# Adaptive-norm scale and shift: from broadcast rows to per-partition scalars at the transposed eviction

## The reference

```python
mod = jax.nn.silu(c) @ w_ada + b_ada
sh1, sc1, g1, sh2, sc2, g2 = [m[:, None, :] for m in jnp.split(mod, 6, axis=-1)]
h = rmsnorm(x, ln_mix_g) * (1.0 + sc1) + sh1
z = h @ w_in
...
x = x + g1 * ((ga * oa + gb * ob + gc * oc) @ w_out)
h2 = rmsnorm(x, ln_ffn_g) * (1.0 + sc2) + sh2
f = moe(h2, router_w, router_b, moe_w1, moe_b1, moe_w2, moe_b2)
x = x + g2 * f
```

## Time and profile before

| what | value |
|---|---|
| median of three runs | 1684.28 us |
| the runs | 1684.28, 1681.4, 1685.1 us |
| span of the profiled execution | 1684.8 us |
| PE busy, share of the span | 1590.9 us, 94% |
| DVE, ACT, POOL busy | 489.1 (29%), 317.7 (19%), 105.6 us (6%) |
| mean granted TensorE clock | 0.962 |
| DMA | 491.89 MB, 292 GB/s over the span |

### The profile page before, as it was taken

The page is one execution under the profiler, slowest core; times in us unless marked ns, Lnnn a source line. Parts: engine busy times, 40 slices in busy tenths (PEclk is TensorE's granted clock), DMA queues, the critical chain, the costliest instruction groups (busy, mean ns, idle before and its releaser), DMA issues.

```text
span 1684.8 us, 20411 instructions
## 1 busy us (share of the span) xinstructions
PE 1590.9 (94%) x8125; PEld 696.9 (41%) x8126; DVE 489.1 (29%) x824; ACT 317.7 (19%) x582; POOL 105.6 (6%) x107
## 2 busy tenths in 40 slices
PE   4989898979999888899999999999999999999996
PEld 4455555444565656233333333333333333333332
DVE  2141222266024645322222222222122222222224
ACT  1123332112121133111111111111111111111120
POOL 0000000112113433000000000000000000000000
PEclk8989999989999888999999999999999999999999
DMA  9462532233223363599999999999593999999993
GB/s 361 170 253 100 204 146 85 103 110 106 94 85 131 103 218 113 221 418 429 429 428 428 429 428 429 429 429 428 244 419 155 417 424 429 428 429 429 428 428 140
DMA packets 38583, 491.89 MB, mean 292 GB/s; under 512 B 4784, under 2 KB 4912, under 8 KB 9744
## 3 DMA queue, kind: packets, MB, share of 16 engines
q1 hardware_dynamic: 34144, 477.27, 68.5%
q0 software_dynamic: 4400, 14.06, 2.9%
HBM read 486.99 MB, written 4.33 MB: 292 GB/s over the span
## 4 chain that ended last, share of the span: by engine, by line
PE 88%; DVE 4%; DMA 4%; ACT 2%; POOL 1%; issue 1%; SPq 0%; DVEq 0%; POOLq 0%
PE ps L1592 28%; PE ps L1264 17%; PE ps L1621 14%; PE ps L1555 6%; PE ps L1541 6%; PE ps L1200 4%; PE ps L1271 4%; DMA ring<-in_w_dense 2%; PE ps L1216 1%; PE ps L1223 1%; PE ps L1597 1%; DMA out_sample_retention<-V 1%; PE ps L1322 1%; PE ps L1342 1%; PE ps L1467 1%
## 5 line engine op out<-in xcount | busy, mean ns | idle before, releaser
L1592 PE MATMUL ps<-ring,arena 128*64 128x512 f32 x2176 | 480.2, 594 | 2.8 <-issue 2.8
L1264 PE MATMUL ps<-ring,xT 128*128 128x512 f32 x672 | 313.0, 624 | 2.9 <-DMA ring<-in_w_dense 2.1
L1592 PEld LDWEIGHTS ps<-ring,arena 128*64 128x64 f32 x2176 | 156.5, 137 | 308.3 <-issue 305.7
L1621 PE MATMUL ps<-ring,arena 128*64 128x512 f32 x1088 | 248.5, 599 | 0.0
L1264 PEld LDWEIGHTS ps<-ring,xT 128*128 128x128 f32 x672 | 131.4, 200 | 165.1 <-issue 160.8
L1178 DVE TENSOR_TENSOR U<-ps,U 128x1024 f32<-128x1024 f32 (+1 forms) x102 | 124.4, 1219 | 248.8 <-PE ps L1555 248.8
L1621 PEld LDWEIGHTS ps<-ring,arena 128*64 128x64 f32 x1088 | 72.0, 137 | 168.1 <-issue 142.3
L1555 PE MATMUL ps<-arena 64*128 64x512 f32 x420 | 119.6, 636 | 0.8 <-ACT arena L734 0.8
L1541 PE MATMUL ps<-T,arena 128*64 128x512 f32 (+1 forms) x420 | 104.4, 616 | 1.2 <-DVE arena L1068 1.2
L1169 DVE TENSOR_SCALAR arena<-ps 128x512 f32<-128x512 f32 x34 | 23.5, 692 | 217.4 <-PE ps L1597 217.4
L707 ACT ACTIVATE W<-ps 128x512 f32<-128x512 f32 x35 | 21.0, 599 | 338.5 <-PE ps L1541 338.5
(11 more groups left out here) (258 smaller groups left out, 1122.9 us busy)
## 6 DMA issues: line engine op xcount, KB each, us to landing
ring<-in_w_moe SPq DMA_DIRECT2D x192, 2048.0 KB, 14.8
ring<-in_w_dense SPq DMA_DIRECT2D x33, 2048.0 KB, 8.8
V<-in_state POOLq DMA_DIRECT2D x8, 256.0 KB, 5.7
out_sample_retention<-V POOLq DMA_DIRECT2D x8, 256.0 KB, 3.1
R<-in_x_prompt SPq DMA_DIRECT2D x1, 1024.0 KB, 16.6
arena<-in_cache_kT POOLq DMA_DIRECT2D x8, 128.0 KB, 3.7
arena<-in_cache_v POOLq DMA_DIRECT2D x8, 128.0 KB, 3.7
arena<-in_b_gate POOLq DMA_DIRECT2D x4, 256.0 KB, 4.0
```

Of the source, the lines that this page charges most:

```text
L1264: last = mm(banks[t][0], xT[:, k, t * P:t * P + P], wv[:, k, :], start=(k == 0), stop=(k == KD - 1))
L1592: last = mm(ps[64 * a:64 * a + 64, half, :], xgT[:, k, j % 2, :], wv[:, k, HALF * a:HALF * a + HALF], start=(j % 2 == 0 and k == 0), stop= ...
L1621: last = mm(ps[64 * a:64 * a + 64, 2, :], actT[:, k, j - 4, :], wv[:, k, HALF * a:HALF * a + HALF], start=(j == 4 and k == 0), stop=(j == ...
```

## The change

Scale and shift are no longer spread to rows. The root still multiplies the token rows, and this scaled x is transposed at once, without gain or shift. Two new transposes per pair of `ada` units (`turn_modulation`) put the model dimension of scale and shift on partitions, and `take_modulation` adds bias and gain there: 128 partitions x 8 chunks x 9 conditions. In the transposed layout the scale and shift of the prompt are one number per partition and chunk. ScalarE (Identity with scale and bias) and VectorE (TENSOR_SCALAR) apply them while they evict the transposed x from PSUM. The sample tile has eight conditions, so VectorE multiplies and adds broadcast views there (`modulated_sample`). `project` takes the chunks in the order in which they are evicted.

SP loads the input, the identity and the parameters ahead of the second unit; bias rows and gain rows are not loaded any more at the start (the bias of the two gates comes later on POOL's queue). The norm before the experts works likewise. Since the gather wants token rows, `xT` is transposed back into `T` (24 transposes, six copies). The spreads of the second gate move from ahead of the expert count to behind the positions.

```diff
-AUX = ["ada2", "ada3"] + [f"gain0{x}" for x in HALVES] + ["ada0", "ada1"] + [f"shift0{x}" for x in HALVES]
-AUX += ["ada4", "ada5", "kT0", "kT1", "kT2"]
+AUX = ["ada2", "ada3", "ada0", "turned2", "ada1", "turned0", "ada4", "ada5", "kT0", "kT1", "kT2"]
 for _t in range(2):
     AUX += [f"qT{_t}{q}" for q in range(4)]
     for _g in range(KVH):
         AUX += [f"sc{_t}{_g}{k}" for k in range(_t + 1)]
+        AUX += {(0, 2): ["turned6"], (1, 0): ["turned8"]}.get((_t, _g), [])
...
+    HAT_BANKS = [1, 3, 0, 2]
+    FIRST_CHUNKS = [4, 5, 6, 7, 0, 1, 2, 3]
+    FFN_BANKS = [1, 3, 0, 2, 4]
+    BACK_BANKS = [(0, 4), (1, 3), (2, 0)]
...
-        for j in range(4):
-            sp.dma_start(mod_bias[32 * j:32 * j + 32], ins["b_ada"][j].partition_broadcast(32)).then_inc(mod_bias_in, 16)
-        load_unit(1)
         sp.dma_start(R[:, 0:2, :], ins["x_prompt"].rearrange("(t p) d -> p t d", p=P)).then_inc(x_in, 16)
         sp.dma_start(R[0:64, 2, :], ins["x_sample"]).then_inc(x_in, 16)
-        sp.dma_start(consts[:, 0:FIRST_CONSTS], ins["consts"][:, 0:FIRST_CONSTS]).then_inc(select_in, 16)
-        sp.dma_start(ln_gain, ins["ln_mix_g"].partition_broadcast(P)).then_inc(ln_mix_in, 16)
+        sp.dma_start(consts[:, 0:IDENT_COLS], ins["consts"][:, 0:IDENT_COLS]).then_inc(ident_in, 16)
+        sp.dma_start(params[:, :], ins["params"]).then_inc(params_in, 16)
+        load_unit(1)
         load_unit(2)
         load_unit(3)
         load_unit(4)
...
+        aux_filled(pool, "ada1")
+        for j in range(4):
+            pool.dma_start(mod_bias[32 * j:32 * j + 32], ins["b_ada"][j].partition_broadcast(32)).then_inc(mod_bias_in, 16)
...
-        take_transposed(0, TR_NORM)
+        act.wait_ge(hat_turned, 1)
+        act.wait_ge(shift_ready, 1)
+        for k in (4, 5, 0, 1):
+            A(xT[:, k, 0:SEQ], ps[:, HAT_BANKS[k // 2], (k % 2) * SEQ:(k % 2 + 1) * SEQ], ACT.Identity,
+              bias=shift_mix[:, k, 0:1], scale=gain_mix[:, k, 0:1]).then_inc(hT_act, 1)
...
-        for x in HALVES:
-            name = f"shift1{x}"
-            aux_filled(act, name)
-            cols = slice(HALF * int(x[1]), HALF * int(x[1]) + HALF)
-            if x[0] == "s":
-                A(T[0:64, 2, cols], aux_bank(name)[0:64], ACT.Copy).then_inc(used(name), 1)
-            else:
-                A(T[:, 0, cols], aux_bank(name), ACT.Copy)
-                A(T[:, 1, cols], aux_bank(name), ACT.Copy).then_inc(used(name), 1)
+        take_transposed(TR_LATER, 4)
+        def take_ffn(t):
+            for q in (2 * t, 2 * t + 1):
+                act.wait_ge(ffn_turned, q + 1)
+                k0 = TR_LATER[q][1]
+                for m in range(4):
+                    last = A(xT[:, k0 + m, t * P:t * P + P], ps[:, FFN_BANKS[q], m * P:m * P + P], ACT.Identity,
+                             bias=shift_ffn[:, k0 + m, 0:1], scale=gain_ffn[:, k0 + m, 0:1])
+                last.then_inc(ffnT_ready, 1)
         for t, pieces in enumerate((2, 1, 1)):
             take_pieces(pieces)
-            if t == 2:
-                take_transposed(2, TR_LATER, 0, 4)
             act.wait_ge(x1_ready, t + 1)
             A(W[0:ROWS[t], t, :], R[0:ROWS[t], t, :], ACT.Square, accum_out=stat[0:ROWS[t], t:t + 1]).then_inc(squared, 1)
             sqrt_of(stat[:, t:t + 1], 12 + t)
-        take_transposed(2, TR_LATER, 4)
+            if t:
+                take_ffn(t - 1)
+        for t, r in enumerate(ROWS):
+            for h in range(2):
+                act.wait_ge(back_turned, 2 * t + h + 1)
+                A(T[0:r, t, HALF * h:HALF * h + HALF], ps[0:r, BACK_BANKS[t][h], :], ACT.Copy).then_inc(back_ready, 1)
...
+            if n in gate_rows:
+                g = gate_rows[n]
+                X.tensor_tensor(mod[:, g, :], aux_bank(name)[:, 0:128], mod_bias[:, g, :], ALU.add).then_inc(used(name), 1)
+            else:
+                X.tensor_copy(mod_rows[:, n % 2, :], aux_bank(name)[:, 0:128]).then_inc(used(name), 1)
+        def take_modulation(n, out, gain=None):
+            name = f"turned{n}"
+            aux_filled(dve, name)
+            turned = aux_bank(name)[:, 0:256].rearrange("p (k b) -> p k b", b=32)[:, :, 0:9]
+            bias = param("ada_bias")[:, 4 * n:4 * n + 8].unsqueeze(2).to_broadcast([P, KD, 9])
+            if gain is None:
+                X.tensor_tensor(out, turned, bias, ALU.add).then_inc(used(name), 1)
+            else:
+                X.tensor_tensor(mod_sum[:, :, :], turned, bias, ALU.add).then_inc(used(name), 1)
+                aux_taken(dve, name)
+                done(X.scalar_tensor_tensor(out=out, in0=mod_sum[:, :, :], scalar=1.0, in1=param(gain).unsqueeze(2).to_broadcast([P, KD, 9]),
+                                            op0=ALU.add, op1=ALU.mult))
+        def modulated_sample(bank, gain, shift, signal):
+            x = ps[:, bank, :].rearrange("p (k b s) -> p k b s", k=KD, b=BATCH_S)
+            h = xT[:, :, SEQ:TOKENS].rearrange("p k (b s) -> p k b s", b=BATCH_S)
+            each = [P, KD, BATCH_S, STEPS]
+            done(X.tensor_tensor(h, x, gain[:, :, 1:9].unsqueeze(3).to_broadcast(each), ALU.mult))
+            X.tensor_tensor(h, h, shift[:, :, 1:9].unsqueeze(3).to_broadcast(each), ALU.add).then_inc(signal, 1)
...
+        dve.wait_ge(squared, 3)
+        root_mean_square(slice(0, 3), 1)
+        for t, r in enumerate(ROWS):
+            X.tensor_scalar(T[0:r, t, :], R[0:r, t, :], stat[0:r, 4 + t:5 + t], None, ALU.mult).then_inc(hat_ready, 1)
+        dve.wait_ge(params_in, 16)
         add_ada_bias(2)
         add_ada_bias(3)
-        dve.wait_ge(squared, 3)
-        root_mean_square(slice(0, 3), 1)
-        dve.wait_ge(ln_mix_in, 16)
-        scale_gain(ln_gain, 0)
-        for t in (2, 0, 1):
-            normalise(t)
+        take_modulation(2, gain_mix, "mix_gain")
         add_ada_bias(0)
         add_ada_bias(1)
-        shift()
-        for x in HALVES:
-            aux_taken(dve, f"shift0{x}")
-        dve.wait_ge(params_in, 16)
+        take_modulation(0, shift_mix)
+        aux_taken(dve, "turned0")
+        dve.sem_inc(shift_ready, 1)
+        dve.wait_ge(hat_turned, 1)
+        for k in (6, 7, 2, 3):
+            X.tensor_scalar(xT[:, k, 0:SEQ], ps[:, HAT_BANKS[k // 2], (k % 2) * SEQ:(k % 2 + 1) * SEQ],
+                            gain_mix[:, k, 0:1], shift_mix[:, k, 0:1], ALU.mult, ALU.add).then_inc(hT_dve, 1)
+        dve.wait_ge(hat_turned, 2)
+        modulated_sample(4, gain_mix, shift_mix, hT_dve)
+        dve.wait_ge(mod_bias_in, 64)
...
+            if ada == 8:
+                take_modulation(6, shift_ffn)
+            if ada == 10:
+                take_modulation(8, gain_ffn, "ffn_gain")
...
-        scale_gain(ln_ffn, 1)
...
-            normalise(t)
-            done(X.tensor_tensor(T[0:r, t, :], W[0:r, t, :], T[0:r, t, :], ALU.add), h_ready)
+            done(X.tensor_scalar(W[0:r, t, :], R[0:r, t, :], stat[0:r, 4 + t:5 + t], None, ALU.mult), h_ready)
+        dve.wait_ge(ffn_turned, 5)
+        modulated_sample(FFN_BANKS[4], gain_ffn, shift_ffn, ffnT_ready)
...
+        def turn_modulation(n):
+            name = f"turned{n}"
+            aux_free(name)
+            for m in range(2):
+                aux_taken(pe, f"ada{n + m}")
+                last = tr(aux_bank(name)[:, m * P:m * P + P], mod_rows[:, m, :], P)
+            last.then_inc(aux_ready, 1)
...
+                    for k in FIRST_CHUNKS:
+                        if idx == 0 and t == 0:
+                            if k // 2 % 2 == 0:
+                                pe.wait_ge(hT_act, 2 if k >= 4 else k + 3)
+                            else:
+                                pe.wait_ge(hT_dve, k - 5 if k >= 4 else k + 1)
+                        last = mm(banks[t][0], xT[:, k, t * P:t * P + P], wv[:, k, :], start=(k == FIRST_CHUNKS[0]), stop=(k == FIRST_CHUNKS[-1]))
                 else:
+                    if idx == 0:
+                        pe.wait_ge(hT_dve, 5)
...
-        for kind, chunks in (("gain0", (2, 3)), ("shift0", (0, 1))):
-            for n in chunks:
-                modulation(n)
-            pe.wait_ge(select_in, 16)
-            for n in chunks:
-                aux_taken(pe, f"ada{n}")
-            spread_halves(kind, chunks[0], HALVES)
-        transpose_all(T, TR_NORM, shifted, 0)
-        pe.wait_ge(xT_ready, 5)
+        modulation(2)
+        pe.wait_ge(ident_in, 16)
+        for t in range(2):
+            pe.wait_ge(hat_ready, t + 1)
+            for k in range(KD):
+                at = (k % 2) * SEQ + t * P
+                last = tr(ps[:, HAT_BANKS[k // 2], at:at + P], T[:, t, k * P:(k + 1) * P], P)
+        last.then_inc(hat_turned, 1)
+        pe.wait_ge(hat_ready, 3)
+        for k in range(KD):
+            last = tr(ps[:, 4, k * 64:k * 64 + 64], T[0:64, 2, k * P:(k + 1) * P], 64)
+        last.then_inc(hat_turned, 1)
+        modulation(3)
+        modulation(0)
+        turn_modulation(2)
+        modulation(1)
+        turn_modulation(0)
...
```

(43 more changed lines are left out.)

84 lines of the change are left out of this document (28 added, 56 removed).

## The result

The changed kernel takes 1665.5 us (median of 6 runs, 1663.4 to 1669.4) against 1682.6 us (6 runs beside it): ratio 0.989, 95% interval 0.987 to 0.992. Run again beside 29 runs of the kernel before it was 0.988 (0.985 to 0.991). The profiled execution has a span of 1664.0 us, 20.8 less than the profile of before.

What follows compares the result with a forecast made beforehand. TensorE was taken to bound the kernel, busy throughout the expert loop, with gains only before it: 9.8 + 3.5 - 0.5 - 0.7 = 12.1 us off the 1684.8 us span, forecast 1672 us, range 1665 to 1679.

Steps and rivals of the forecast that it cites:

- the way home before the experts: Between last router product and gather: transposing h back to token rows makes 11.95 us into 14.0, 2.0 us lost.
- The start: Up to the first projection matmul: fewer queued bytes and no spreads bring it from 47.3 to 37.5 us, 9.8 gained.
- The clock at the first projection: First projection: without spreads ahead it starts at the lower clock level, 0.7 us lost, between nothing and 1.7.
- The restart of 1.7 us: After a starved stretch: 32 projection matmuls took 15.70 us instead of 14.0, read as a restart's cost of 1.7 us.
- The attention stage: Attention: four extra transposes in TensorE's order cost 0.5 us, bounds 0 and 1.2.
- Before the experts: Output projection to expert loop: 5.5 us gained up to the last router product, 2.0 lost behind it, net 3.5.
- Up to the last router product: Before the experts: the last router product ends at 660.0 us against 665.52, 5.5 us gained, bounds 4.8 and 6.8.
- (1) The way home eats the second stage: Before the experts: slow transposes and spreads, blocked residuals, nothing gained after the projection; 1675.7 us, chance 0.15.
- (2) Bytes do not count: Start: only the number of transfers sets when ada1's weights land, 6.3 us gained there; 1675.7 us, chance 0.06.
- (3) The whole first piece at the lower level: First projection piece: all runs at 1.2 GHz, 7.0 us more instead of 0.7; 1678.5 us, chance 0.10.
- (4) The loop gives the lead back: Expert loop: tied to its weight loads, so the edit does nothing; 1684 us, chance 0.06.
- (5) Projections stay slow: Early projections: stay at 1.2 GHz, 0.438 us more per matmul, two whole units give 1700 us; chance 0.05.

Runs made afterwards that it cites:

- rows back: Changed kernel with three 512 KB row loads that nobody reads put on SP's queue ahead of the second modulation unit; 1668.7 us, ratio 0.993.
- start only: Kernel before with only the mixing norm changed, the norm before the experts left as it was; 1679.9 us, ratio 0.996.
- no way home: Changed kernel without the 24 transposes back and six copies, gate spreads ahead of the routing wait as in the kernel before; 1670.0 us, ratio 0.993.
- half units: Changed kernel with its first projection unit loaded as two transfers, the half used first ahead; 1665.9 us, ratio 0.991.
- both: Changed kernel with evictions before the experts split between ScalarE and VectorE, sample piece first, and first projection unit loaded in two halves; 1661.4 us, ratio 0.989.
- shared: Changed kernel with chunks 4 to 7 of each prompt tile evicted on VectorE and the sample piece ahead on ScalarE; 1659.6 us, ratio 0.986.
- spreads behind: Changed kernel without the 24 transposes back and six copies, gate spreads kept behind the positions; 1666.6 us, ratio 0.991.

## Why it came out so, step by step

The direction held. The terms for start, clock and the stage before the experts came to 15.7 us where the prediction had 9.8 - 0.7 + 3.5 = 12.6. One step had the wrong sign, the way home before the experts.

**The start.** Predicted 9.8 us, measured 11.4 (A, both pairs). ada1 landed at 30.2, not 32.1. The price per byte was right (rows back: 3.68 us for 1536 KB); beyond it, the first modulation began 1.06 us earlier (9.47 against 10.53), and some 0.9 us of the 5.4 stay unexplained. From there to the first projection 5.4 us were forecast (3.39 + 2.0), and 5.7 and 5.8 passed, but not by the forecast's steps: in the first trace modulation 1 took 1.95 us and the projection then waited for its own weights, which were to have come first; in the second modulation 1 took 3.46 us and the evictions ended last.

**The clock at the first projection.** Predicted -0.7, measured -1.4 and -1.7 (B). It is not a fixed cost: start only, no way home and half units have the same transposes and modulations ahead and show none; rows back shows 3.0. Half units and both have the same wait of 1.59 us in front, and took 13.97 and 15.67. The restart of 1.7 us read from the earlier trace rows is no fixed price either: in the second trace of the kernel before the same 32 matmuls took 14.00 us. The granted clock is recorded as 1.00 in the 24 transposes at the start and 0.50 in the first projection matmuls behind the 2.98 us wait:

```profile
20.58:25.16 4.58, 4.58 (x24) 4.17 (x24) 1.36 (x3) 0.00 (x0) 0.00 (x0) 1.00 1.01 429
...
35.87:38.50 2.63, 2.63 (x3) 1.17 (x4) 0.67 (x1) 0.00 (x0) 1.44 (x3) 0.50 1.10 391
```

The fall comes at the end of the wait (0.91 from 33.00 to 35.80 us) and behind it, and with the wait filled it is gone in both kernels that do so; but three of the nine traces with the new start and no fill don't have it either, so two traces prove little here, and what decides it stays open. The 1.00 of the first line does not fit the pace: these transposes took 4.66 us, about as long as the 24 of the way home that began at 0.50 (4.73), and 4.18 us in the second trace at a recorded mean of 0.60. The Trainium skill (TensorE: Matmul & The Clock Gate, Part 4: PE-mode transpose) says transposes do not count as busy work for the clock as matmuls do. By it the fall would be the transposes' doing; the first line can't decide that, and the two stretches of transposes in the last section speak against it.

**The attention stage.** Predicted -0.5; not measurable, since C differs by up to 13.1 us between traces of one program. Whether any of the 6.4 us between the first two profiles are the edit's work, no run could show.

**Before the experts.** This is the step that failed. Predicted +3.5; measured with the loop's first unit 90.25 and 90.68 before [81.47 + 8.78, 81.90 + 8.78] against 85.74 and 83.66 after, 5.8 in the mean. Its parts:

- Up to the last router product 5.5 us were forecast. From the start of the output projection it took 60.6 and 61.2 us before, 57.1 and 55.5 after: 3.4 to 5.7. The evictions were mis-sized (2.9 us a tile instead of 2.0), and they were on the path: shared, D falls. The second tile's router product was priced at 1.9 us and took 3.62 in both traces, at a granted 0.50 behind the wait of 4.62 and 4.09. The second tile's residual, priced at 1.4 free and 4.0 blocked, took 2.56 (1.15 and 1.41, each begun beside a GpSimd cast; the lines stand last).
- "I take 14.0, so 2.0 us lost" had the wrong sign, and of all steps it is off by most. Router to loop was 20.9 and 20.8 us before, 18.8 and 18.5 after: 2.0 to 2.4 gained. The prediction added the way home to the path and priced the spreads at their old 6.03 us. In fact transposes and spreads went into waits that TensorE had in any case, and what stands behind ran at a granted 1.00: spreads 3.94 us, gather 2.94.
- Not foreseen: the loop's first unit took 9.83 and 9.68 us instead of 8.78. The granted clock of the block it opens is 0.90 against 0.94, and filling the wait in front brought it to 7.09. Why the same wait costs more in the changed kernel stays open: without the way home it was 8.74 us with the spreads behind the positions and 9.78 with them ahead.

In sum 11.4 - 1.5 + 5.8 = 15.7 us by these three stages, against 12.6 (12.1 with the attention stage). The medians differ by 17 to 20; the other 1 to 5 us are smaller than what C does from run to run, and no run says where they come from.

**The rivals.** (1) The way home eats the second stage: refuted by no way home and, with the spreads left in their place, by spreads behind. (2) Bytes do not count: refuted by rows back. (3) The whole first piece at the lower level: 1.4 to 1.7 us of the 7.0 came. (4) The loop gives the lead back: the steady part is unchanged. (5) Projections stay slow: B is 1.4 to 1.7 us longer and no more.

**What it said would show.** First projection at 36 to 39 us: 35.87. ada1 near 32: 30.2. Lead unchanged at 600 us: no, C swings. Last router product some 15 us earlier: 19.7, with C's share. Gather to loop unchanged: no, 7.5 us instead of 9.0. Two of the signs that it named against itself are there: narrow evictions ending a tile's wait, and a granted clock under 1.00 in the first projection unit (0.50 in its first 2.6 us).

## What to carry to other kernels

An operation that is added in front of a wait on another engine need not be added to the path: ask first what the engine would do in that time. On TensorE it may even pay twice, because an idle stretch can be paid again behind it in slower matmuls, as in the loop's first unit (9.31 us, and 7.09 with the wait filled). A gain in one stage is judged by the length of that stage, in two traces of each kernel, before any difference elsewhere is explained.

## What the runs showed of the hardware

The granted clock falls at other places in each execution of one program: stage C took 262.4 and 275.5 us at a mean of 0.94 and 0.90. One and the same sample piece, in the first and in the second trace:

```profile
272.38 3.67 PE L1293 MATMUL ps<-ring,xT 128*64 128x256 f32 x32
280.35 6.41 PE L1293 MATMUL ps<-ring,xT 128*64 128x256 f32 x32
```

The clock also rose while TensorE did nothing but transposes. The way home of the changed kernel by stretches:

```profile
645.79:648.00 2.21, 2.21 (x12) 2.21 (x12) 1.83 (x13) 0.80 (x2) 0.00 (x0) 0.50 0.00 0
648.00:649.00 1.00, 1.00 (x6) 1.00 (x5) 0.96 (x2) 0.74 (x2) 0.00 (x0) 0.50 0.00 0
649.00:650.00 1.00, 1.00 (x8) 0.89 (x7) 0.40 (x1) 0.74 (x2) 0.00 (x0) 0.64 0.06 16
650.00:651.00 1.00, 1.00 (x11) 0.96 (x9) 0.00 (x0) 0.98 (x3) 0.00 (x0) 1.00 0.00 0
```

From 0.50 it goes through 0.64 to 1.00 between 649 and 650 us, and the counting matmuls begin only at 650.36.

In the second trace of the changed kernel the same shows at the start, where TensorE has nothing to do from 12.76 to 19.82 us and then the 24 transposes, with the next modulation behind them at 23.93:

```profile
12.80:19.80 7.00, 0.00 (x0) 0.01 (x1) 1.22 (x4) 4.72 (x8) 0.00 (x0) 0.75 1.03 420
19.82:20.50 0.68, 0.68 (x4) 0.68 (x5) 0.68 (x2) 0.00 (x0) 0.00 (x0) 0.50 0.96 410
22.50:23.00 0.50, 0.50 (x4) 0.50 (x3) 0.00 (x0) 0.00 (x0) 0.00 (x0) 0.50 1.00 426
23.00:23.93 0.93, 0.93 (x11) 0.65 (x9) 0.00 (x0) 0.00 (x0) 0.00 (x0) 0.94 1.04 440
```

The residual's operations that ran beside GpSimd can be priced from the traces. On VectorE and on GpSimd, in the changed kernel:

```profile
623.84 1.15 DVE L1059 TENSOR_TENSOR W<-W,V 128x512 f32<-128x512 f32 x1 [2.47 <-ACT W L553]
625.02 1.41 DVE L1060 TENSOR_TENSOR R<-R,W 128x512 f32<-128x512 f32 x1
```

```profile
623.41 1.03 POOL L500 CAST consts<-U 32x1024 bf16<-32x1024 f32 x1
624.50 1.38 POOL L501 CAST consts<-U 32x1024 bf16<-32x1024 f32 x1
```

Each ends 0.55 us after the GpSimd operation under which it began (624.99 and 624.44; 626.43 and 625.88). In the kernel before it was 0.56 (643.01 and 642.45). With GpSimd idle such an operation took 0.69 us.
